# A one-core diffusion-step kernel: two of four latent tiles of the expert layer by a streamed table and dense gates instead of per-token gathers

## The chip, the cores and the metric

The kernel runs on one core of one Trainium2 chip. The metric is device time in microseconds (us), and lower is better. Everything is float32. Three runs of the kernel before gave 2536.47 us (median), 2534.52 and 2538.31.

## The reference, cut to what matters

One layer of a diffusion backbone over 128 context tokens and 512 latent tokens, 1024 wide. A mixing part (a gated recurrence plus attention) adds `y` to `x`; then comes PEER, an expert layer over 16384 experts, which is what the change is about. `w_u` and `w_v` are tables of 16384 rows of 1024 numbers (64 MB each).

```python
def peer(h, w_q, sub_keys, w_u, w_v):            # per block of 128 tokens
    q = (xb @ w_q).reshape(n, P_HEADS, 2, P_QDIM // 2)        # 8 heads
    s = jnp.einsum('nhpd,hpkd->nhpk', q, sub_keys)            # 2 x 128 scores a head
    s1, i1 = lax.top_k(s[:, :, 0], 16)
    s2, i2 = lax.top_k(s[:, :, 1], 16)
    cand_s = s1[..., :, None] + s2[..., None, :]
    cand_i = i1[..., :, None] * 128 + i2[..., None, :]
    top_s, pos = lax.top_k(cand_s, 16)
    idx = jnp.take_along_axis(cand_i, pos, axis=-1)           # 16 experts a head and token
    g = jax.nn.softmax(top_s, axis=-1)
    act = jax.nn.gelu(jnp.einsum('nhkd,nd->nhk', w_u[idx], xb))
    return jnp.einsum('nhk,nhkd->nd', g * act, w_v[idx])
x = x + gate1 * y;  x = x + gate2 * peer(rmsnorm(x) * (1 + scale2) + shift2)
```

A tile is 128 tokens: tile 0 is the context, tiles 1 to 4 are the latents. Each token picks 8 x 16 = 128 experts, so a tile needs 128 "slots" of 128 rows of both tables.

## The kernel before, in words

**Tiles and order.** The program is one hand-ordered stream per engine. `plan_groups` lists every PSUM group (`NAMES`) in the order in which TensorE makes it; the other engines walk the same list. The order is: modulation vectors (`ada`), the context tile's mixing part, its `post(0)`, the latent tiles' projections and mixing (`mix(1)`), then `post(1)` for tile 1 and `post(2)` for tiles 2 to 4. `post` multiplies by `w_out` (groups `y`), normalizes, turns (`x2T`, `h2`), and makes the queries (`qp`) and scores (`ss`) of the 8 heads. PA has four PSUM banks, taken in turn.

**Slots.** A slot is one indirect DMA of 1 MB (`gather`: for each of 128 tokens a row of `u` and a row of `v` side by side, array `uv`), a dot product of the `u` half with the token's `h2` on VectorE (`dot`, L1412), a GELU and a weight on ScalarE (`w_slot`, L957, L963), and an accumulation of the weighted `v` half. For tile 0 the last is a scalar-tensor-tensor on VectorE into PSUM (`v_row`, L1440). For the other tiles TensorE does it: ScalarE makes a diagonal matrix of the weights (L973) and two matmuls of 512 columns add into PSUM (`v_slot`, L600); of tile 1's first 64 slots every second goes this way (`v_odd`, L587). Gathers are issued by GpSimd (L1213, L1235). In all 640 slots.

**Placing.** `Beside` puts slots between the groups of the list at places that `STAGES` sets: tile 0's 128 slots beside projections, attention and `mix(1)`, then 64 slots of tile 1 beside the two posts. The other 448 slots follow in loops with no other work, with eight gather buffers (`GB_`: the three slab slots, HL, and `GA`); beside other work there are four (`GA`) or six (`GC`).

**Routing.** For each head VectorE finds the 16 experts in about 30 small instructions (`route_parts`, L1332 to L1389): two top-16 searches over 128 scores, 54 candidate sums, a third search, and three passes over 128 x 864 elements that turn positions into expert numbers. It is cut into 12 parts laid between the slots (`ROUTE_AT`); after part 7 ScalarE takes the exponentials (L952). `tile_end` adds the result to `x`, normalizes and hands the tile to the output DMA.

**Slabs.** SP streams all weights as slabs of 1 MB through a ring of three (`SLABS`, `NSLAB`); a slab's DMA is issued when the slab three before it has been read.

## Time and profile before

| | before |
|---|---|
| median of 3 runs | 2536.47 us |
| runs | 2534.52 to 2538.31 us |
| profiled execution, span of its records | 2543.3 us |
| busy TensorE / VectorE / ScalarE / GpSimd | 79% / 69% / 37% / 37% |
| DMA moved | 805.53 MB, mean 317 GB/s |

### The profile page before, as it was taken

To read this page: it belongs to the slowest core of one execution; us is meant where nothing else is said; L and a number is where in the kernel's file an instruction comes from. 1 tells how busy PE (TensorE), PEld (TensorE's weight loads), DVE (VectorE), ACT (ScalarE), POOL (GpSimd) and SP (SyncE) were. 2 spreads that over 40 slices of the span, in tenths; PEclk is the share of its full clock that TensorE was granted. 3 is DMA by queue.
4 is the path that set the end of the run, shared out by engine and by line. 5 is a ranking of instruction groups with operands and counts; after the bars stand their busy time and mean duration, and the time that the engine had idled before them with its cause. 6 is when DMAs were issued, how large, how long until landed. Compare 5 with 4: busy or idle time off the path is not lost. (4 is left out here: it accounts for less than half of the span.)

```text
span 2543.3 us, 27323 instructions
## 1 busy us (share of the span) xinstructions
PE 2005.6 (79%) x6925; PEld 1104.9 (43%) x6925; DVE 1749.4 (69%) x3969; ACT 945.2 (37%) x2456; POOL 941.2 (37%) x774
## 2 busy tenths in 40 slices
PE   6978898946677798668698776877768787687876
PEld 2577846745566543267455222322223222232222
DVE  2732278886776678767787777777777777777764
ACT  1402145223343434312333444444444444344443
POOL 0020012232222222303233554656545665456654
PEclk9998999977888899879899998999999999999999
DMA  8744678851111389859798999999999999999997
GB/s 317 289 152 154 231 291 322 332 192 67 67 67 60 150 332 337 337 203 401 272 372 317 422 421 393 420 422 422 421 404 415 422 422 421 407 401 421 422 422 330
DMA packets 113299, 805.53 MB, mean 317 GB/s; under 512 B 12596, under 2 KB 14006, under 8 KB 17046
## 3 DMA queue, kind: packets, MB, share of 16 engines
q0 software_dynamic: 93760, 680.96, 66.5%
q1 hardware_dynamic: 17704, 118.17, 12.6%
q10 hardware_dynamic: 1712, 4.98, 0.5%
q8 instruction: 50, 0.82, 0.1%
q14 instruction: 73, 0.60, 0.1%
HBM read 800.79 MB, written 3.28 MB: 316 GB/s over the span
## 5 line engine op out<-in xcount | busy, mean ns | idle before, releaser
L1213 POOL DMA_INDIRECT RG<-in_uv,idxs x264 | 356.5, 1351 | 562.0 <-DVE pl L1440 322.1
L957 ACT ACTIVATE agel<-apre 128x1 f32<-128x1 f32 x640 | 129.3, 202 | 984.6 <-DVE apre L1412 981.2
L600 PE MATMUL pl<-RG,BP 128*128 128x512 f32 x576 | 294.9, 638 | 106.8 <-ACT BP L973 102.3
L600 PE MATMUL pl<-RING,BP 128*128 128x512 f32 x576 | 281.7, 621 | 62.1 <-ACT BP L973 59.6
L1412 DVE CUSTOM_DVE_ANT_0 R<-RG,AB 128x1024 f32<-128x1024 f32 x201 | 246.8, 1230 | 100.8 <-DMA RG<-in_uv,idxs 79.8
L1213 POOL DMA_INDIRECT RING<-in_uv,idxs x168 | 248.9, 1482 | 158.7 <-PE pl L600 69.4
L1412 DVE CUSTOM_DVE_ANT_0 R<-RING,AB 128x1024 f32<-128x1024 f32 x168 | 205.9, 1226 | 95.6 <-DMA RING<-in_uv,idxs 77.2
L625 PE MATMUL pa<-HL,RING 128*128 128x512 f32 (+2 forms) x800 | 243.7, 461 | 4.2 <-DVEq L457 2.6
L600 PEld LDWEIGHTS pl<-RG,BP 128*128 128x128 f32 x576 | 100.1, 192 | 294.5 <-ACT BP L973 214.0
L973 ACT ACTIVATE BP<-CT,wexp 128x128 f32<-128x128 f32 x480 | 192.7, 401 | 51.1 <-PE pl L600 12.9
L600 PEld LDWEIGHTS pl<-RING,BP 128*128 128x128 f32 x576 | 104.3, 194 | 234.2 <-ACT BP L973 139.7
L963 ACT ACTIVATE wexp<-agel,gws 128x1 f32<-128x1 f32 x640 | 188.7, 295 | 22.4 <-ACT agel L957 0.3
L625 PEld LDWEIGHTS pa<-HL,RING 128*128 128x128 f32 x800 | 134.5, 195 | 106.0 <-issue 74.3
L1213 POOL DMA_INDIRECT EB<-in_uv,idxs x88 | 118.3, 1345 | 147.0 <-DVE pl L1440 96.8
L1440 DVE SCALAR_TENSOR_TENSOR pl<-RG,wexp,pl 128x1024 f32<-128x1024 f32 x118 | 151.6, 1285 | 9.6 <-ACT wexp L963 9.5
L1412 DVE CUSTOM_DVE_ANT_0 R<-RG,BP 128x1024 f32<-128x1024 f32 x96 | 117.7, 1226 | 43.4 <-DMA RG<-in_uv,idxs 27.6
L1412 DVE CUSTOM_DVE_ANT_0 R<-EB,AB 128x1024 f32<-128x1024 f32 x67 | 82.4, 1229 | 60.1 <-DMA EB<-in_uv,idxs 58.0
L625 PE MATMUL pa<-RING,AB 128*128 128x256 f32 (+2 forms) x432 | 103.9, 390 | 14.8 <-DVEq L457 10.3
L600 PE MATMUL pl<-HL,BP 128*128 128x512 f32 x192 | 94.9, 617 | 24.9 <-ACT BP L973 22.2
L957 ACT ACT_TABLE_LOAD x86 | 110.3, 1283 | 9.9 <-ACT RING L1096 2.8
L600 PE MATMUL pl<-EB,BP 128*128 128x512 f32 x192 | 98.8, 639 | 11.1 <-ACT BP L973 11.1
L625 PEld LDWEIGHTS pa<-RING,AB 128*128 128x128 f32 (+1 forms) x432 | 82.9, 201 | 34.1 <-issue 17.3
(288 smaller groups left out, 3261.0 us busy)
## 6 DMA issues: line engine op xcount, KB each, us to landing
RING<-in_in_slabs SPq DMA_DIRECT2D x42, 1024.0 KB, 6.0
RING<-in_pq_slabs SPq DMA_DIRECT2D x24, 1152.0 KB, 5.5
RING<-in_ada_slabs SPq DMA_DIRECT2D x16, 1024.0 KB, 5.0
RING<-in_out_slabs SPq DMA_DIRECT2D x12, 1024.0 KB, 9.1
RG<-in_col_slabs POOLq DMA_DIRECT2D x8, 1024.0 KB, 6.9
RING<-in_o_slabs SPq DMA_DIRECT2D x8, 1024.0 KB
RG<-in_uv,idxs POOLq DMA_INDIRECT x297
RING<-in_uv,idxs POOLq DMA_INDIRECT x168
```

What stands on the lines that cost most here:

```text
L600: last = nc.tensor.matmul(acc[:, c * 512:(c + 1) * 512], DG[:, k % 2, :], bufs[k % len(bufs)][:, D + c * 512:D + (c + 1) * 512], start=Fal ...
L625: return nc.tensor.matmul(out, l, r, start=s, stop=e)
L957: A(agel[:, par, k:k + 1], apre[:, par, k:k + 1], ACT.Gelu).then_inc(gel_done, 1)
L963: A(wexp[:, par, k:k + 1], agel[:, par, k:k + 1], ACT.Copy, scale=gws[:, par, k:k + 1]).then_inc(w_done, 1)
L973: A(DG[:, i % 2, :], ident, ACT.Copy, scale=wexp[:, par, k:k + 1]).then_inc(dg_done, 1)
L1213: nc.gpsimd.indirect_dma_start(out=bufs[b], out_offset=None, in_=uv, in_offset=bass.IndirectOffsetOnAxis(ap=idxs[:, par, k:k + 1], axis=0) ...
L1412: V.tensor_tensor_reduce(out=SCR[k % 2], in0=buf[:, 0:D], in1=hc, scale=1.0, scalar=0.0, op0=ALU.mult, op1=ALU.add, accum_out=apre[:, par, ...
L1440: V.scalar_tensor_tensor(PL[:, :], (GC[i % NGC] if t else GA[n % NGA])[:, D:2 * D], wexp[:, n // TOPK % 2, n % TOPK:n % TOPK + 1], PL[:, : ...
```

## The change

Tiles 0, 1 and 3 keep the gathers. Tiles 2 and 4 are computed densely: for every one of the 16384 experts, whether a token picked it or not.

- **Table.** `u_slabs` and `v_slabs` are the two tables cut into 128 chunks of 128 experts, two chunks to a slab of 1 MB: 64 `dU` and 64 `dV` slabs through the same ring. `experts_u(c)` (group `("U", c)`) multiplies a chunk with the 256 tokens of both tiles (8 matmuls of 256 columns); `gelu_u` puts GELU of it into `AR`, a ring of 50 chunks. `weigh` multiplies 16 chunks by their gates. `experts_v(c)` (`("V", c)`, L994) adds chunk c's part of both outputs into PSUM (4 matmuls of 512 columns).
- **Gates.** The dense gate of (token, expert) is the softmax weight or 0. Sixteen `dense_route` calls (one per head of tiles 2 and 4) are whole routings on VectorE, in a workspace of their own (`WD`, in `mbias`). Then, per token, a one-hot matrix of each slot's first key times its weight (`OH1`, 8 tensor-scalars of 128 x 128 per 8 tokens on GpSimd, `slot_hots`; for every second group of tile 4 on VectorE, `drawn`) and one of its second key (`OH2`, one 128 x 1024 comparison per 8 tokens on VectorE, `gate_hots`) are multiplied on TensorE (groups `G`, four tokens each, 64 groups). ScalarE copies them to staging (`gates_out`) and writes them to an array in HBM (16 DMAs of 1 MB in pieces of 1 KB), from which SP reads 16 blocks of 1 MB back (`gate_slab`).
- **Slots.** 384 instead of 640, all with `v_row` on VectorE; for tiles 1 and 3 it accumulates in SBUF (`ACC`). No diagonal matrices, no slot matmuls, no loops. All gathers have four buffers (`GA`, `GD`).
- **Order.** Tile 0's end now stands ahead of `post(1)`. The posts are for tiles 1, 2 and 3, 4. Scores are copied out of PSUM by ScalarE, not VectorE. Three dense routings stand between the posts, with no slots in `post(1)`; 26 slots beside `post(2)`; 24 beside the new stage `early` (U chunks 0 to 49, all of the gates, 13 dense routings); 206 beside the new stage `dense` (128 V chunks and U chunks 50 to 127). The ends of tiles 3, 2 and 4 follow in a row.
- **Spill.** `x` of tiles 1 to 4 is written to HBM in the posts and read back for the tile's end (`x1s`).

```diff
-NGA, NGC, NGB = 4, 6, 8
+NGA, NGD = 4, 4
+DENSE, GATHERED = (2, 4), (0, 1, 3)
+NCH, NEARLY, NRING = NKEYS, 34, 50
-BATCHES = [(0,), (1,), (2, 3, 4)]
+BATCHES = [(0,), (1, 2), (3, 4)]
...
-          ("post1", 0, {"y": 3.5, "x2T": 2.0, "h2": 2.0, "qp": 2.0, "ss": 1.0}),
-          ("queries1", 4, {"qp": 2.0, "ss": 0.1}),
-          ("post2", 60, {"y": 3.4, "x2T": 2.5, "h2": 2.5, "qp": 5.2, "ss": 1.2}))
+          ("post1", 0, {}),
+          ("post2", 26, {"y": 3.4, "x2T": 2.5, "h2": 2.5, "qp": 5.2, "ss": 1.2}),
+          ("early", 24, {"U": 3.4, "T": 1.0, "G": 1.6}),
+          ("dense", 206, {"V": 1.0, "U": 1.0}))
...
+SLABS += [("dU", p) for p in range(NRING // 2)]
+for _p in range(NCH // 2):
+    SLABS += [("dV", _p)] + ([("dU", _p + NRING // 2)] if _p + NRING // 2 < NCH // 2 else [])
+DENSE_AT = {("U", 2 * (d - NAHEAD)) if d < PH else ("G", 0, 4 * (d - PH)): d for d in range(NAHEAD, 2 * PH)}
...
+            def experts_u(c):
+                w = slab("dU", c // 2)[:, c % 2 * D:(c % 2 + 1) * D]
+                ps = start(("U", c))
+                for k in range(KD):
+                    last = mm(ps[:, 0:DTOK].rearrange("p (t n) -> p t n", t=ND), w[:, k * P:(k + 1) * P],
+                              hTl[:, k, :].rearrange("p (t a n) -> p t a n", t=ND, a=2)[:, :, 1, :], k == 0, k == KD - 1)
...
+            def experts_v(c):
+                w = slab("dV", c // 2)[:, c % 2 * D:(c % 2 + 1) * D]
+                if c % GBLK == 0:
+                    pe.wait_ge(p_done, ND * (c // GBLK + 1))
+                for i in range(ND):
+                    for x in range(2):
+                        last = nc.tensor.matmul(VACC[i][:, x * 512:(x + 1) * 512], AR[:, c % NRING, i * P:(i + 1) * P],
+                                                w[:, x * 512:(x + 1) * 512], start=c == 0, stop=c == NCH - 1,
+                                                skip_group_check=True)
...
+            def dense_route(d):
+                t, h = DHEADS[d]
+                b = 1 if t in BATCHES[1] else 2
+                dve.wait_ge(sc_ready, 2 * PH * b + 2 * h + 2)
+                for i in range(10):
+                    search(WD, t, h, i)
+                    if i == 3 and d % PH:
+                        weights_of(d - 1)
+                    if i == 7:
+                        dve.sem_inc(dlogit_ready, 1)
+                r(V.tensor_reduce(slots_at(d, 2), REQ, AX, ALU.add))
...
+                for x in range(ONEHOT):
+                    at = q * ONEHOT + x
+                    step.post(nc.gpsimd.tensor_scalar(OH1[n % 2][:, x, :], iota_p, SLT[i][:, 0, at:at + 1],
+                                                      SLT[i][:, 2, at:at + 1], ALU.is_equal, ALU.mult))
...
+            tile_end(0)
+            post(1)
+            route(PH, 0, 12)
+            route(PH + 1, 0, EARLY)
+            for d in range(NAHEAD):
+                dense_route(d)
+            beside.open(1)
+            post(2)
+            for name in early_order():
+                if name in DENSE_AT:
+                    dense_route(DENSE_AT[name])
+                if name[0] == "G" and name[2] % 2 == 0:
+                    gate_hots(name[1], name[2] // 2)
```

TensorE at the end of the program: `po` and `pl` are PSUM accumulators, `BP` holds the diagonal matrices, `RING`, `RG`, `HL` and `EB` gather buffers. Before, the last rows of the last loop's tail:

```order
L600 MATMUL pl<-RING,BP 128x512 x6
L600 MATMUL pl<-HL,BP 128x512 x2
L600 MATMUL pl<-RG,BP 128x512 x6
L600 MATMUL pl<-EB,BP 128x512 x2
L894 MATMUL pl<-ZB 128x128 x8
```

In the change, from the middle of the stage `dense` (`AB` is the ring of weighted activations, `RING` the slabs):

```order
L994 MATMUL pl<-RING,AB 128x512 x2
L710 MATMUL pa<-HL,RING 128x256 x16
L994 MATMUL po<-RING,AB 128x512 x2
L994 MATMUL pl<-RING,AB 128x512 x2
L994 MATMUL po<-RING,AB 128x512 x2
L994 MATMUL pl<-RING,AB 128x512 x2
```

A slot no longer has a matmul; two V chunks and two U chunks take turns.

VectorE before, in a gather loop (`ISA` is the dot product and the read of its sum, the rest are parts of a routing):

```order
L1412 ISA R,apre<-HL,AB 128x1024
L1412 ISA apre 128x1
L1375 TENSOR_TENSOR BP<-BP 128x864
L1412 ISA R,apre<-RG,AB 128x1024
L1412 ISA apre 128x1
L1377 TENSOR_REDUCE BP<-BP 128x16
L1379 CAST idxs<-BP 128x16
```

In the change, in the stage `early`, the end of a dense routing (`CT`), a one-hot comparison (`XS`), a slot, and a part of a slot's routing (`BP`):

```order
L1493 TENSOR_SCALAR CT<-CT 128x1
L1495 CAST CT<-CT 128x16
L1496 TENSOR_TENSOR BP<-CT 128x864
L1499 TENSOR_TENSOR BP<-BP,CT 128x864
L1540 TENSOR_REDUCE BP<-BP 128x16
L1567 TENSOR_TENSOR XS<-CT,BP 128x1024
L1593 ISA R,apre<-R,BP 128x1024
L1593 ISA apre 128x1
L1619 SCALAR_TENSOR_TENSOR AB<-R,wexp,AB 128x1024
L1469 TENSOR_TENSOR BP<-BP 128x2x12
```

Dense routings and comparisons stand on VectorE in one piece between slots, and the accumulation (L1619) has moved to VectorE with its sum in SBUF.

## Rows read from the trace of the kernel before

**Rows 1.** The page, 40 slices of 63.6 us each: busy tenths and GB/s.
```profile
PE   6978898946677798668698776877768787687876
DVE  2732278886776678767787777777777777777764
DMA  8744678851111389859798999999999999999997
GB/s 317 289 152 154 231 291 322 332 192 67 67 67 60 150 332 337 337 203 401 272 372 317 422 421 393 420 422 422 421 404 415 422 422 421 407 401 421 422 422 330
```
**Rows 2.** Windows: window, length, then busy us (count) of PE, PEld, DVE, ACT, POOL, PEclk, DMA share, GB/s.
```profile
900.00:1096.00 196.00, 150.69 (x343) 65.44 (x342) 155.70 (x241) 74.27 (x152) 54.80 (x49) 0.90 0.86 326
1144.00:1208.00 64.00, 56.16 (x269) 45.33 (x268) 49.06 (x124) 15.41 (x46) 20.59 (x20) 0.95 0.99 401
1270.00:1330.00 60.00, 60.00 (x207) 35.28 (x206) 49.71 (x114) 19.04 (x58) 19.30 (x18) 1.00 0.96 370
1500.00:2300.00 800.00, 623.41 (x1300) 228.56 (x1300) 585.26 (x1435) 350.19 (x1030) 454.20 (x313) 0.96 1.00 414
```
**Rows 3.** ScalarE groups in the window 1500 to 2300 us: count of slots.
```profile
L957 ACT ACTIVATE agel<-apre 128x1 f32<-128x1 f32 x313 | 63.1, 202 | 381.3 <-DVE apre L1412 380.3
```
**Rows 4.** VectorE timeline: start, us, engine, line, idle before; slots beside `mix(1)`, then end of them.
```profile
1056.06 1.23 DVE L1412 CUSTOM_DVE_ANT_0 R<-RG,BP 128x1024 f32<-128x1024 f32 x1 [1.40 <-DMA RG<-in_uv,idxs]
...
1058.49 1.22 DVE L1412 CUSTOM_DVE_ANT_0 R<-RG,BP 128x1024 f32<-128x1024 f32 x1
...
1094.67 1.23 DVE L1412 CUSTOM_DVE_ANT_0 R<-EB,BP 128x1024 f32<-128x1024 f32 x1 [0.26 <-DVE AB L1683]
...
1100.88 0.42 DVE L1719 TENSOR_TENSOR HG<-pa,G1L 128x256 f32<-128x256 f32 x1 [3.77 <-PE pa L625]
...
1104.33 0.42 DVE L1719 TENSOR_TENSOR HG<-pa,G1L 128x256 f32<-128x256 f32 x1 [2.46 <-PE pa L625]
```
**Rows 5.** TensorE timeline in `mix(1)`: 32 matmul instructions of 512 columns.
```profile
959.51 14.32 PE L625 MATMUL pa<-HL,RING 128*128 128x512 f32 x32 [0.19 <-ACTq L457]
```
**Rows 6.** Lines L1719 and L1744 (first to last start), then score copies of `post(0)`.
```profile
L1719 DVE TENSOR_TENSOR HG<-pa,EB x4: 425/425/426, 266.3 to 276.6; 128x256 f32<-128x256 f32 x4
L1744 DVE COPY R<-pa x32: 278/292/292, 292.5 to 1388.3; 128x128 f32<-128x128 f32 x32
...
302.54 0.29 DVE L1744 COPY R<-pa 128x128 f32<-128x128 f32 x1 [1.72 <-PE pa L625]
304.55 0.29 DVE L1744 COPY R<-pa 128x128 f32<-128x128 f32 x1 [1.72 <-PE pa L625]
```
**Rows 7.** VectorE timeline of a whole routing on its own: first and last of its rows.
```profile
323.14 0.29 DVE L1350 COPY BP<-R 128x256 f32<-128x256 f32 x1
323.58 0.29 DVE L1332 MAX8 BP<-BP 128x8 f32<-128x128 f32 x1
...
336.09 0.23 DVE L1389 TENSOR_SCALAR gws<-BP 128x16 f32<-128x16 f32 x1
```
**Rows 8.** Groups by shape: VectorE over 128x1024, GpSimd over 128x128, gathers by GpSimd.
```profile
L1699 DVE TENSOR_TENSOR AB<-AB,R 128x1024 f32<-128x1024 f32 x4 | 4.9, 1225 | 0.6 <-DVE R L1698 0.3
L1706 DVE SCALAR_TENSOR_TENSOR AB<-AB,st,R 128x1024 f32<-128x1024 f32 x4 | 5.1, 1284 | 1.1 <-DMA R<-in_normf_rows 1.0
L1255 POOL TENSOR_TENSOR HG<-HG 128x128 f32<-128x128 f32 x5 | 2.3, 468 | 0.4
L1213 POOL DMA_INDIRECT RG<-in_uv,idxs x45: 932/1643/1917, 1599.9 to 1882.8; - x45
```
**Rows 9.** Timeline at the end of the program.
```profile
2529.48 1.23 DVE L1412 CUSTOM_DVE_ANT_0 R<-EB,AB 128x1024 f32<-128x1024 f32 x1 [1.22 <-DMA EB<-in_uv,idxs]
2534.30 1.23 DVE L1698 TENSOR_TENSOR R<-pl,G 128x1024 f32<-128x1024 f32 x1 [3.59 <-PE pl L894]
...
2540.24 0.33 SPq L570 DMA_DIRECT2D out<-AB  x1
```

More of the change, by code:

```diff
@@ L78 @@
 EARLY = 6
-FIRST_ODD = 9
 EXPO_AT = 5
@@ L475, in open, with clear @@
             def open(self, t):
-                self.first, self.end = t * TSLOT, min((t + 1) * TSLOT, NSLOT)
+                self.first, self.end = (0, TSLOT) if t == 0 else (TSLOT, NSLOT)
+            def clear(self):
+                while self.next < self.end and self.next % TOPK in (3, 4):
+                    self.slot(self.next)
+                    self.next += 1
             def rest(self):
@@ L1838, in shape_constants @@
+            beside.before(("U", NRING - 4))
+            weigh(0, 0)
+            weigh(0, 1)
+            beside.before(("V", 4))
+            weigh(1, 0)
+            weigh(1, 1)
+            for b in range(2, NBLK):
+                beside.before(("V", GBLK * b - 8))
+                weigh(b, 0)
+                weigh(b, 1)
+            beside.rest()
+            for e in range(2, NT):
+                tile_end(e)
 def shape_constants():
```

775 lines of the change are left out of this document (425 added, 350 removed).

## The prediction, made before the changed kernel was run

> **What bounds the kernel now.** I read the 40 slices first. From slice 23 on, 1400 us into the span, DMA stands at 9 and moves 393 to 422 GB/s, while VectorE and TensorE stand at 7 [rows 1]. Before that no stage holds DMA at its limit for long. The windows say the same in numbers: from 1500 to 2300 us the DMA share is 1.00 at 414 GB/s, TensorE is busy 623 of 800 us and VectorE 585 [rows 2]. In that window 313 slots pass, one per 2.56 us [rows 3], and each is 1.049 MB, so the last 45% of the program is a gather stream and nothing else counts there. The reader should see that taking bytes away pays here, and only as long as the other two engines, at 78% and 73%, don't become the bound. Beside other work the picture is another: from 900 to 1096 us (`mix(1)`, four gather buffers and the slab ring, as in the whole changed kernel) the DMA share is 0.86 at 326 GB/s with no engine over 80%; from 1144 to 1208 us slabs and gathers together reach 401 GB/s at share 0.99; from 1270 to 1330 us TensorE is the bound and DMA moves 370 [rows 2]. These rates price the new stages.
>
> **Bytes.** 256 slots of 1.049 MB go (268 MB). The table brings 128 slabs (134 MB), the gates 16 MB units out and 16 back (34 MB), the spill of x 4 MB. Net 96 MB less; at 414 GB/s that is 232 us, the most the change could give if DMA stayed the bound throughout. It doesn't, so I sum the stages.
>
> **Up to the posts: nothing.** The slots of tile 0 keep their places, so the first `y` matmul of `post(1)` starts where it did, one group ahead of its first reader: 1100.88 - 3.45 = 1097.4 us (the pitch of these groups is 1104.33 - 1100.88) [rows 4]. Tile 0's end now stands ahead of that reader on VectorE: after the last dot product at 1094.67 us [rows 4], one accumulation (1.28) and a tile end, 2540.24 - 2534.30 = 5.9 us [rows 9]. I cost it at nothing: four PSUM banks take four `y` groups, 13.8 us, before TensorE is stopped. Were that cover gone, it would cost 7 us. The removed score copies free VectorE but stand beside TensorE's work: nothing.
>
> **post(1), 106 us.** Eight `y` groups by 3.45: 28. Then norm, turns and first query: in `post(0)` 292.5 - 276.6 = 15.9 us pass from the last `y` to the first score, of which two pitches (4.0) are queries: 12 for one tile [rows 6], 15 for two. A head half of `post(0)` has 16 + 2 instructions of 128 columns in 2.01 us [rows 6], 0.11 each; one of 256 columns takes 3.45/16 = 0.22. So 16 x 0.22 + 4 x 0.11 = 3.9 us, sixteen times: 63. VectorE meanwhile does the first routing of tile 1, half the second and three dense ones. A whole routing alone takes 336.32 - 323.58 = 12.7 us [rows 7]; a dense one lacks a cast, 12.4. That is 57 us beside the 63. Ends at 1203.
>
> **post(2), 118 us.** The same 28 + 15. Beside the queries each pair of head halves needs 1.18 MB of slab and 2.4 gathers, 3.7 MB: 9.3 us at 401 GB/s, against 7.9 of TensorE and, by 3.2 us a slot, 8 of VectorE. A slot alone costs VectorE 1058.49 - 1056.06 = 2.43 us [rows 4]; its share of a routing is 12.5/16 = 0.8. So 75 us, and 1321.
>
> **early, 344 us.** Here VectorE is the bound, and this is the price of the change. Chunks 0 to 9 carry five dense routings (62) and three slots (10): 72, where TensorE needs 35. Tile 2's gates: eight routings (99), sixteen comparisons of 128 x 1024 at 1.23 [rows 8] (20), nine slots (29), turning the slots (3): 151. Tile 4's gates: sixteen comparisons (20), eight drawn pairs at 2.5 (20), eight slots (26): 66, TensorE 62. Then sixteen U chunks by TensorE: 16 x 3.45 = 55. The DMA need (25 slabs, 24 gathers, 16 gate writes) is 65 MB units, 170 us, so half of DMA's time is given away here. The gate writes go in pieces of 1 KB; no row shows such a write, and even at twice the time per byte they hide (16 x 2.6 us more of 170 idle). The Trainium skill ("Perfetto Trace Analysis", DMA Optimizations) says that transfers under 2 KB carry significant overhead each and speaks for larger ones; by it the 170 grow and the sum stays. Ends at 1665.
>
> **dense, 845 us.** 206 gathers less 3 already issued, 100 slabs, 12 gate reads, 2 units of x: 317 x 1.049 = 332 MB. At 401 GB/s 829 us. TensorE: a 512-column instruction takes 14.32/32 = 0.45 us [rows 5], so a V chunk (8) 3.6 and a U chunk 3.45: 128 x 3.6 + 78 x 3.45 = 727. VectorE: 206 x 2.43 + 11 routings (138) + 14 weighings of 2048 columns (34) + one tile end (8) = 681. The accumulation in SBUF instead of PSUM costs no more: 1284 ns with all operands in SBUF [rows 8]. DMA is last, but by 12% only. I add 2 us at each of eight gate blocks, where V waits for `weigh`: 845. Bounds: 332/0.414 = 803 and 332/0.326 = 1020; I take the row in which both queues were backlogged, since three engines with room keep them so. Ends at 2510.
>
> **Tail, 23 us.** Last dot 1.2, accumulation 1.3, three tile ends at 5.9, output 3.1 (2540.24 to the end) [rows 9]; before, it was 2543.3 - 2529.5 = 14.
>
> Sum 1097 + 106 + 118 + 344 + 845 + 23 = 2533 against a span of 2543.3. Measured runs lie 6.8 us under the span: 2527, or 0.4% faster. A 96 MB saving comes to 10 us, because early stands still for DMA. The break-even is dense at 855 us, 389 GB/s.
>
> **Rivals.**
> **1. Coupling (slower).** In dense a slot stands at every chunk, four buffers hold the gathers, and V waits for gates every 16 chunks. Each engine is within 18% of the longest, and a late one holds the rest. For it: in 900 to 1096 us, built the same way, 326 GB/s with room on all engines [rows 2]. Against it: V chunks need no reply from VectorE within a block, and TensorE may run four U groups ahead. At 370 GB/s dense takes 898 us, the kernel 2580; it decides from 389 down. At 326 it would be 2700.
> **2. GpSimd in early (slower).** 192 tensor-scalars of 128 x 128 lie there. The nearest row is 468 ns [rows 8], 3.7 us per 8 tokens, hidden. But a gather's issue spreads from 0.93 to 1.92 us beside VectorE's slots [rows 8]: if each small operation were held 1.0 us so too, 8 tokens take 11.8 us. Tile 2's gates would take 188 + 9 issues of 1.9 = 205 instead of 151, tile 4's 94 + 15 = 109 instead of 66: 97 more, 2624. The Trainium skill ("SBUF — State Buffer", SBUF: two separate sides) says that a VectorE operation with two SBUF inputs and a GpSimd operation that reads SBUF lock each other out for a whole instruction; by it this rival is the rule.
> **3. DMA stays full (faster).** Slabs as large as the gathers at the pure gather rate, 414 GB/s, and no block waits: dense 803, the kernel 2485.
>
> **How the numbers follow.** Forecast 0.48, rival 1 0.22, rival 2 0.12, rival 3 0.18. 0.2% (5 us) is about what a measurement tells from no change. The forecast's own range is 2500 to 2560 (early and posts 15 us either way, dense 829 to 860): 0.34 faster, 0.08 same, 0.06 slower. Rival 3 is faster; rival 1 gives 0.02 to same and 0.20 to slower; rival 2 is slower. Faster 0.52, same 0.10, slower 0.38. The range reaches from below rival 3 (2455, with early 30 us shorter as well) to 2610, past rival 1 at 370 GB/s; the worst of rivals 1 and 2 stay out.
>
> **What would show it.** Right: VectorE at 9 through early and DMA near half; early 330 to 360 us long; in dense a DMA share of 0.97 or more near 400 GB/s, a slot per 4.1 us, TensorE waiting for slabs and VectorE for gathers. Rival 1: DMA share near 0.9, waits of GpSimd on the accumulation and of TensorE on ScalarE or VectorE. Rival 2: GpSimd full in early and TensorE's G groups waiting for it. It would be wrong altogether if the posts, with ScalarE now copying scores, waited for ScalarE, or if a dense routing took longer than 12.4 us for its waits on the exponential.

## The result, and where the time went

| | before | after |
|---|---|---|
| median of the runs | 2535.5 us (2533.6 to 2538.3) | 2725.1 us (2719.5 to 2728.9) |
| profiled span | 2543.3 us | 2727.0 us |

The ratio of after to before is 1.0741, with a 95% interval of 1.0725 to 1.0757. The changed kernel is 7.4% slower. 2527 us and a range up to 2610 were predicted. The bytes came out as reckoned: DMA moved 707.90 MB, 98 MB less than before, where 96 had been forecast. The time did not follow them.

The page of the changed kernel, busy tenths in 40 slices of 68.2 us, answers to [rows 1]:

```profile
PE   6969899566777984956844467899878787879772
DVE  3642388877766887348687765466676867676767
POOL 0020022222221222001207778322222222222221
DMA  8826598721114897435933445689989899999986
GB/s 310 302 104 232 205 361 333 270 73 62 62 62 183 337 342 271 183 134 219 366 107 105 142 162 193 251 323 388 392 345 393 330 397 351 398 360 382 377 337 239
```

The flat row of 9s that the kernel before had is gone. In slices 17 to 19, the posts, DMA is at 3 to 5; in slices 21 to 25, the early stage, at 3 to 5 again, and GpSimd stands at 7 and 8 in slices 22 to 25, while VectorE falls from 8 to 4 (slices 21 to 26). Later DMA comes back to 330 to 398 GB/s, not to 420.

The stages as I had summed them, by first and last instructions in the trace (first reader of `y`, first gelu of a U chunk, first V matmul, last accumulation of a slot):

| | posts | early | dense | from start to posts | tail |
|---|---|---|---|---|---|
| predicted | 224 | 344 | 845 | 1097 | 23 |
| after | 275 | 429 | 911 | 1090 | 22 |
| difference | +51 | +85 | +66 | -7 | -1 |

Three stages miss by 51, 85 and 66 us, and with the other two that is all of the 194 us between a span of 2533 and one of 2727. As forecast, tile 0's end cost nothing (the first reader of `y` comes 3.6 us late behind it, and from the third on VectorE waits for TensorE again), and the tail took 22.

These marks lie later than the prediction's, which counts a stage from its first matmul. TensorE's first `y` matmul is at 1079.7 us, its first U matmul at 1347.7, while ScalarE stood for a dense routing (8.3 us) before its exponential and came to the first gelu only at 1365.0:

```profile
1347.70 13.98 PE L710 MATMUL pa<-HL,RING 128*128 128x256 f32 x64
```

By the prediction's own marks the start is 18 us early, the posts take 268 us (44 over) and early 446 (102 over); the sum is the same. The first reader of `y` lies anywhere between 1088 and 1104 us in the profiles of this kernel and of its variants, none of which differs before it, so a shift of the start by 15 us means nothing.

**The posts.** VectorE's waits from 1125 to 1240 us, TensorE's from 1187 to 1300:

```profile
DVE BP L1514 <- ACT BP L1063: 40.9, 1, 40.9
DVE BP L1459 <- ACTq L530: 14.2, 1, 14.2
...
PE pa L710 <- DVEq L530: 35.0, 1, 35.0
PE pa L713 <- DVEq L530: 17.0, 1, 17.0
```

L1514 is part 11 of the first gathered routing of tile 1, L1063 its exponential. The two timelines, VectorE's and ScalarE's, show why it is late:

```profile
1187.27 0.16 DVE L1514 RECIPROCAL BP<-BP 128x1 f32<-128x1 f32 x1 [40.93 <-ACT BP L1063]
...
1185.09 0.27 ACT L1257 ACTIVATE AB<-pa 128x128 f32<-128x128 f32 x1
1185.54 1.28 ACT L1063 ACT_TABLE_LOAD   x1 [0.17 <-ACT AB L1257]
1186.84 0.31 ACT L1063 ACTIVATE BP<-BP 128x16 f32<-128x16 f32 x1
```

The exponential stands in ScalarE's program behind all 16 query and score groups of `post(1)`, of which the last copy (L1257) is at 1185.09. VectorE reached it at 1146 and stood still. Its three dense routings, which I had laid beside TensorE's queries, then came after the queries; TensorE made the first four `y` groups of `post(2)`, one for each bank, and waited 35.0 us for VectorE to read them.

**Early.** Windows: chunks 0 to 9, tile 2's gates, tile 4's gates, the last sixteen U chunks. Columns as in [rows 2].

```profile
1363.00:1440.00 77.00, 27.83 (x99) 22.45 (x99) 62.32 (x216) 20.92 (x39) 10.44 (x13) 0.71 0.31 109
1440.00:1610.00 170.00, 97.68 (x483) 87.81 (x483) 126.31 (x340) 53.41 (x97) 126.81 (x128) 0.79 0.41 135
1610.00:1735.00 125.00, 76.83 (x400) 70.70 (x401) 66.05 (x81) 26.03 (x55) 96.95 (x72) 0.80 0.54 179
1735.00:1793.00 58.00, 58.00 (x270) 51.07 (x269) 22.51 (x30) 9.01 (x27) 5.76 (x5) 1.00 0.82 313
```

I had 72, 151, 66 and 55. Two thirds of the excess is in tile 4's gates (59 of 86 us), where VectorE, said to be the bound, is busy 66 of 125 us and GpSimd 97. The one-hots that GpSimd scales, by source line (shortest, median and longest ns, first and last start):

```profile
L1384 POOL TENSOR_SCALAR EB<-CT,BP x128: 780/791/2544, 1433.1 to 1597.7; 128x128 f32<-128x128 f32 x128
L1384 POOL TENSOR_SCALAR EB<-CT,RW x64: 785/1402/2542, 1610.9 to 1724.8; 128x128 f32<-128x128 f32 x64
```

GpSimd's timeline, one piece in each part:

```profile
1468.12 7.98 POOL L1384 TENSOR_SCALAR EB<-CT,BP 128x128 f32<-128x128 f32 x8
...
1625.68 10.87 POOL L1384 TENSOR_SCALAR EB<-CT,RW 128x128 f32<-128x128 f32 x8 [2.08 <-PE pa L710]
1637.45 1.02 POOL L1371 DMA_INDIRECT R<-in_uv,idxs  x1 [0.91 <-POOL EB L1384]
```

One takes 0.78 us at least, where I had 0.47 from the nearest row; eight take 7.98 us beside the end of one slot and a routing's small instructions, and 10.87 beside comparisons and a slot, all of 1024 columns. TensorE waits 48.3 us in eight pieces for GpSimd in 1600 to 1735.

A second price hangs on these waits. TensorE does the `G` groups of tile 4 in eight pieces of four groups, 32 matmul instructions each. Two of them:

```profile
1621.79 6.74 PE L710 MATMUL pa<-XS,EB 128*128 128x128 f32 x32 [11.93 <-POOLq L530]
1681.73 3.84 PE L710 MATMUL pa<-XS,EB 128*128 128x128 f32 x32 [1.55 <-POOLq L530]
```

After the wait of 11.9 us the granted clock was 0.53 over the piece (1621.8 to 1628.3), close to the lower of its two levels, 1.2 GHz; after the wait of 1.55 it was 1.00. Seven of the eight pieces follow waits of 4.7 to 11.9 us and take 5.3 to 6.7 us. All eight take 45.9 us, where 3.84 each would be 31: 15 us more, in the same chain with GpSimd's pieces. The forecast priced TensorE at its full clock everywhere.

**Dense.** Two windows, same columns:

```profile
1850.00:2100.00 250.00, 219.65 (x727) 142.35 (x726) 173.68 (x301) 47.26 (x156) 55.82 (x55) 0.95 0.96 378
2100.00:2450.00 350.00, 282.93 (x920) 180.27 (x918) 258.29 (x440) 63.66 (x213) 88.21 (x79) 0.95 0.95 368
```

DMA moves 368 to 378 GB/s, not 401; over the whole stage 332 MB in 911 us are 365. No engine is full. The waits in 1850 to 2450 us form a circle: GpSimd waits for VectorE's accumulation, VectorE for gathers, and TensorE for ScalarE.

```profile
POOL R L1371 <- DVE AB L1619: 328.5, 97, 11.9
POOL AB L1371 <- DVE AB L1619: 112.3, 31, 5.9
...
DVE R L1593 <- DMA R<-in_uv,idxs: 90.0, 48, 4.1
DVE R L1593 <- issue: 36.3, 19, 3.8
DVE R L1593 <- DMA AB<-in_uv,idxs: 20.0, 13, 4.2
...
PE pa L710 <- ACTq L530: 89.6, 35, 10.0
```

From this profile alone one can't say which link of it is the tight one.

### The profile page after: what moved, and what is told of

It is laid out like the page before. It is cut to its first block, busy times and chain, and to the rows that moved or that the text cites. A ratio compares the mean times of both kernels' runs of the same rounds, so it can differ in the third digit from the quotient of the medians.

```text
span 2727.0 us, 28055 instructions
## 1 busy us (share of the span) xinstructions
PE 2068.6 (76%) x8515; PEld 1459.6 (54%) x8515; DVE 1809.1 (66%) x3622; ACT 701.7 (26%) x1719; POOL 714.1 (26%) x713
## 2 busy tenths in 40 slices
DMA packets 114558, 707.90 MB, mean 260 GB/s; under 512 B 11140, under 2 KB 28934, under 8 KB 32614
## 4 chain that ended last, share of the span: by engine, by line
DMA 27%; DVE 26%; PE 21%; issue 16%; POOL 7%; ACT 2%; DVEq 1%; POOLq 0%; ACTq 0%; SPq 0%
DMA R<-in_uv,idxs 21%; PE pa L710 18%; POOL EB L1384 6%; DVE AB L1619 5%; DVE pl L1619 4%; DMA AB<-in_uv,idxs 3%; DVE AB L1584 2%; PE po L710 1%; PE pa L713 1%; DVE AB L1748 1%; DVE AB L1756 1%; DMA EB<-in_uv,idxs 1%; DMA RING<-in_ada_slabs 1%; DVE BP L1499 1%; DVE BP L1496 1%
## 5 line engine op out<-in xcount | busy, mean ns | idle before, releaser
L710 PE MATMUL pa<-HL,RING 128*128 128x256 f32 (+1 forms) x2848 | 731.2, 416 | 120.6 <-ACTq L530 116.5
L710 PEld LDWEIGHTS pa<-HL,RING 128*128 128x128 f32 x2848 | 557.5, 199 | 294.4 <-issue 222.0
L1371 POOL DMA_INDIRECT R<-in_uv,idxs x288 | 322.2, 1119 | 1150.5 <-DVE AB L1619 736.0
L1593 DVE CUSTOM_DVE_ANT_0 R<-R,BP 128x1024 f32<-128x1024 f32 x192 | 235.5, 1227 | 134.6 <-DMA R<-in_uv,idxs 90.6
L1619 DVE SCALAR_TENSOR_TENSOR AB<-R,wexp,AB 128x1024 f32<-128x1024 f32 x192 | 246.0, 1281 | 54.4 <-ACT wexp L1081 54.2
L994 PE MATMUL po<-RING,AB 128*128 128x512 f32 x512 | 244.3, 600 | 39.6 <-DVEq L1586 39.6
L994 PE MATMUL pl<-RING,AB 128*128 128x512 f32 x512 | 243.0, 597 | 0.0
L710 PE MATMUL pa<-RING,AB 128*128 128x256 f32 (+3 forms) x528 | 125.0, 386 | 80.8 <-DVEq L530 77.1
L994 PEld LDWEIGHTS po<-RING,AB 128*128 128x128 f32 x512 | 98.1, 192 | 147.1 <-issue 145.0
L994 PEld LDWEIGHTS pl<-RING,AB 128*128 128x128 f32 x512 | 98.5, 192 | 124.6 <-issue 124.6
L1384 POOL TENSOR_SCALAR EB<-CT,BP 128x128 f32<-128x128 f32 x128 | 124.8, 984 | 18.7 <-PE pa L710 16.9
L1371 POOL DMA_INDIRECT AB<-in_uv,idxs x64 | 63.6, 994 | 251.6 <-DVE AB L1619 243.0
L1619 DVE SCALAR_TENSOR_TENSOR pl<-R,wexp,pl 128x1024 f32<-128x1024 f32 x96 | 123.3, 1285 | 5.5 <-ACT wexp L1081 5.3
```

The costliest lines, as they stand in the source:

```text
L710: return nc.tensor.matmul(out, l, r, start=s, stop=e)
L994: last = nc.tensor.matmul(VACC[i][:, x * 512:(x + 1) * 512], AR[:, c % NRING, i * P:(i + 1) * P], w[:, x * 512:(x + 1) * 512], start=c == ...
L1371: nc.gpsimd.indirect_dma_start(out=bufs[b], out_offset=None, in_=uv, in_offset=bass.IndirectOffsetOnAxis(ap=idxs[:, par, k:k + 1], axis=0) ...
L1384: step.post(nc.gpsimd.tensor_scalar(OH1[n % 2][:, x, :], iota_p, SLT[i][:, 0, at:at + 1], SLT[i][:, 2, at:at + 1], ALU.is_equal, ALU.mult))
L1593: V.tensor_tensor_reduce(out=SCR[k % 2], in0=bufs[b][:, 0:D], in1=hc, scale=1.0, scalar=0.0, op0=ALU.mult, op1=ALU.add, accum_out=apre[:, ...
L1619: V.scalar_tensor_tensor(acc, (GD[(n - TSLOT) % NGD] if s else GA[n % NGA])[:, D:2 * D], wexp[:, n // TOPK % 2, n % TOPK:n % TOPK + 1], ac ...
```

## The experiments

All stand on the changed kernel unless said otherwise. Stage lengths in us, by the same marks:

| run | posts | early | dense | median | to before (95%) |
|---|---|---|---|---|---|
| after | 275 | 429 | 911 | 2725.1 | 1.0725 to 1.0757 |
| e1_expos | 232 | 433 | 910 | 2694.6 | 1.059 to 1.065 |
| e2_hots | 275 | 399 | 902 | 2695.5 | 1.059 to 1.066 |
| e3_noslots | 273 | 363 | 992 | 2742.3 | 1.077 to 1.083 |
| e4_small_slabs | 271 | 434 | 809 | 2634.8 | 1.033 to 1.040 |
| e5_pattern | 274 | 428 | 912 | 2729.4 | 1.066 to 1.077 |
| e6_few_rows | 274 | 435 | 789 | 2613.4 | 1.023 to 1.031 |
| e7_light_pe | 273 | 435 | 913 | 2739.6 | 1.072 to 1.081 |
| e8_light_dve | 276 | 429 | 848 | 2671.0 | 1.046 to 1.055 |
| e9_ring42 | 275 | 423 | 907 | 2724.5 | 1.072 to 1.076 |
| e10_five | 273 | 421 | 842 | 2653.3 | 1.044 to 1.048 |
| e11_combo | 235 | 399 | 907 | 2660.0 | 1.046 to 1.050 |
| e12_all | 230 | 388 | 843 | 2588.0 | 1.018 to 1.024 |
| e13_half_pool | 272 | 379 | 902 | 2673.0 | 1.050 to 1.057 |
| e14_scalar_hots | 235 | 381 | 841 | 2579.6 | 1.013 to 1.019 |
| e15_scalar_hots_split | 234 | 373 | 847 | 2570.2 | 1.008 to 1.015 |
| e16_more_early | 237 | 401 | 803 | 2559.3 | 1.006 to 1.010 |
| e17_eight_early | 235 | 384 | 822 | 2559.1 | 1.008 to 1.012 |

### The posts: e1_expos

```diff
                 for m in range(2 * PH):
+                    if b == 1 and m in (6, 11, 15):
+                        x = (6, 11, 15).index(m)
+                        expos(PH) if x == 0 else dense_expos(x - 1)
                     ps = group(("qp", b, m))
...
-            expos(PH)
-            for d in range(NAHEAD):
+            for d in range(2, NAHEAD):
                 dense_expos(d)
```

> Correct kernel. ScalarE takes the exponential of the first gathered routing after post(1)'s sixth query group and those of the first two dense routings after the 11th and 15th, instead of all of them after the 16 groups. Theory (the wait of VectorE on ScalarE between the posts is on the path: 40.9 us at 1187, after which TensorE waits 35.0 us at 1233 for VectorE): post(2) starts about 35 to 40 us earlier, the stages behind it keep their lengths, and the time falls by 30 to 45 us, to about 2685. Rival (the wait only hides work that has to be done anyway, and post(2) or the early stage takes it back): the time falls by under 10 us. Second rival: ScalarE now stands still in post(1) for the logits, and post(1) becomes longer by what it waits, so that the gain is 15 to 25 us.

Measured: 31 us less, the posts 43 us shorter, early and dense as long as before within 4 us. (Between the two profiled spans, 2727.0 and 2695.3, the difference to 43 is a start 8 us later and 4 us in early.) VectorE's waits from 1130 to 1240 us, TensorE's from 1190 to 1290, in the new profile:

```profile
DVE BP L1462 <- ACTq L531: 13.3, 1, 13.3
DVE st L1654 <- ACTq L531: 2.7, 1, 2.7
DVE BP L1517 <- ACT BP L1064: 1.2, 1, 1.2
...
PE pa L714 <- DVEq L531: 15.0, 1, 15.0
PE pa L711 <- ACTq L531: 1.5, 2, 0.9
```

The wait of 40.9 is 1.2 and TensorE's 35.0 is gone. What is left of the posts, 232, is 8 from the 224 predicted; by the prediction's marks it is 226 (1087.7 to 1313.8 us). The theory stands.

### Early: e2_hots, e3_noslots, e5_pattern, e13_half_pool

e2: VectorE makes all first one-hots of tile 4.

```diff
-            return i == ND - 1 and q % 2 == 1
+            return i == ND - 1
```

> Correct kernel. All of tile 4's first one-hots (16 groups of 8 tokens) are made by VectorE, where the change has GpSimd make every second group; GpSimd's 64 instructions that took 1.40 us on average are gone, VectorE gets 8 more pairs of 1.25 and 1.36 us, 21 us. Theory (GpSimd sets the pace of tile 4's gates, 122 us long): VectorE then is busy some 87 us there, TensorE 77, and the stage takes 90 to 100 us; the time falls by 22 to 32 us. Rival (the pace there is set by the slots in VectorE's order and their gathers, GpSimd only follows): the stage gets 15 to 20 us longer, and the time with it.

Measured: 30 us less. Tile 4's gates, from first comparison to last gate copy, go from 121 to 89 us. The window over them in e2, beside the third of the windows of early above:

```profile
1617.00:1706.00 89.00, 67.86 (x387) 61.15 (x388) 81.58 (x92) 25.23 (x54) 8.80 (x7) 0.87 0.65 220
```

VectorE is now busy 82 of 89 us: this is the stage as I had meant it, only with more work on VectorE. GpSimd had been the pace. TensorE gains too: its waits are short, the granted clock is 0.87 instead of 0.80, and it is busy 68 us instead of 77.

e3: no slot in early, 230 in dense (the count of `early` in `STAGES` 0, of `dense` 230).

> Correct kernel. No slot lies in the early stage; its 24 go to the dense stage (230 instead of 206). Theory (GpSimd's scalings are slow because VectorE works beside them on two operands from SBUF; alone one takes 0.79 us): without the slots GpSimd's mean stays above 1.0 us in tile 2's gates, since the comparisons of VectorE remain, and falls in tile 4's; the early stage gets 40 to 70 us shorter (VectorE loses 24 slots of 2.5 us and their waits), and the dense stage longer by 24 slots of 4.4 us, 106, so the time rises by 35 to 65 us. Rival (the dense stage is bound by DMA at its own rate, and 24 MB more cost 24 x 1.05 MB / 0.401 = 63 us there): the time is the same within 15 us.

Measured: 17 us more, under the theory's 35 to 65 and just past the rival's 15. Early is 65 us shorter, so a slot costs 2.7 us there, and dense 81 us longer, 3.4 a slot. Slots aren't cheaper in early than 2.7, although DMA is idle half the time. GpSimd's mean goes from 1.40 to 1.18 us in tile 4's gates, as expected; in tile 2's it goes from 0.98 to 0.95, so it was never above the 1.0 that the expectation names.

e5: the same number of drawn groups, in another pattern.

```diff
-            return i == ND - 1 and q % 2 == 1
+            return i == ND - 1 and q % 4 in (1, 2)
```

> Correct kernel. In tile 4's gates VectorE makes the first one-hots of the groups of tokens 1, 2, 5, 6, 9, 10, 13, 14 instead of 1, 3, 5, ...: as many as before on either engine, but GpSimd's eight now fall on both buffers instead of always on the same one. Theory (the price of tile 4's gates is a chain in series: 8 scalings of GpSimd, 10.9 us, then the 4 us in which TensorE reads that buffer, eight times 15): GpSimd's work overlaps TensorE's, the stage falls from 121 us to 85 to 100, and the time by 20 to 35 us. Rival (GpSimd's sum, 89 us busy with the gathers' issues, and its lock-outs by VectorE set the pace whatever the buffers): the stage keeps 110 us or more, and the time falls by under 10 us.

A miss for the theory, as its rival had it: 2729.4 us, no change (121 to 115 us in that part). Its timeline shows GpSimd's two pieces of eight now one after the other, with the wait for TensorE between them:

```profile
1620.82 10.83 POOL L1388 TENSOR_SCALAR EB<-CT,RW 128x128 f32<-128x128 f32 x8 [11.41 <-ACTq L530]
1632.56 1.01 POOL L1375 DMA_INDIRECT R<-in_uv,idxs  x1 [0.91 <-POOL EB L1388]
1638.48 10.45 POOL L1388 TENSOR_SCALAR EB<-CT,RW 128x128 f32<-128x128 f32 x8 [4.91 <-PE pa L714]
```

So the price isn't the order in which the two buffers are filled. GpSimd's piece takes 10.5 to 10.9 us in either order.

e13: GpSimd makes 4 of each 8.

> The output is not the reference's: GpSimd makes only every second of its scaled one-hots (96 of 192), the others keep what stood in the buffer; all else is the changed kernel. It asks what GpSimd's work costs in each part of early. Theory (GpSimd's 8 scalings, 7.8 us per 8 tokens in tile 2's gates, run against VectorE's 9 us and the two are coupled through two buffers; in tile 4's they stand in series with TensorE's reading, 10.9 + 4): tile 2's gates fall from 162 us (first to last comparison 151.6) by 10 to 25 us, since VectorE's 148 us stay, and tile 4's from 121 to 85 to 95; the time falls by 40 to 60 us. Rival (in tile 2's gates GpSimd is hidden and VectorE alone is the pace): only tile 4's part falls, and the time by 25 to 35 us.

Measured: 52 us less. Tile 2's gates, from their first comparison to the first of tile 4's, go from 165 to 154 us; tile 4's, from there to the last gate copy, from 121 to 83. Both fell, as the theory has it: half of GpSimd's work costs 11 us in tile 2's gates and 38 in tile 4's. The 38 hold the clock's part as well: over tile 4's gates the granted clock rises from 0.80 to 0.90, and TensorE is busy 64 us instead of 77. With that half gone, tile 2's part is at 154, against 151 predicted from VectorE's sum.

### Dense: e4_small_slabs, e6_few_rows, e7_light_pe, e8_light_dve

e4 and e6 bring less of each slab of the dense stage:

```diff
+                if kind == "dV" or (kind == "dU" and key[1] >= NRING // 2):
+                    at, src = at[0:8], src[0:8]
```

(e4: `[:, 0:SLAB // 4]` instead.)

> The output is not the reference's: the slabs of the tables that the dense stage reads (all of V's, and U's last 39) bring only the first quarter of their columns, the rest of each buffer keeps what was there; every instruction, wait and gather remains. 103 MB of the dense stage's 340 shrink to 27 MB. Theory (the coupling of VectorE's slots, ScalarE's order and the gathers' four buffers sets the pace, the queues only follow): the dense stage of 911 us keeps 850 us or more, and the time falls by under 60 us. Rival (the DMA engines are the bound, at a lower rate for slabs and gathers mixed than for gathers alone): the stage goes in proportion to its bytes until TensorE, 711 us busy, or VectorE, 655, bounds it, to 720 to 780 us; the time falls by 130 to 190 us.

> The output is not the reference's: the slabs that the dense stage reads bring 8 of their 128 partitions, in full rows of 8 KB (with a quarter of the columns for all partitions the DMA share had stayed at 0.88 at 320 GB/s, since the pieces became 2 KB). 97 MB of the dense stage's 340 go. Theory (what is left when DMA is no bound is TensorE's 3.44 us per V and U chunk in the first part, 537 us, VectorE's some 3.9 us per slot in the V-only part, about 190, and their coupling): V's first to last matmul takes 740 to 785 us instead of 882, the DMA share falls below 0.75, and the time falls by 95 to 145 us. Rival (the coupling alone is the pace, the quarter slabs gained by something else): under 60 us.

Measured: 90 and 112 us less. e4 lies between its two theories; its DMA share stayed at 0.87 to 0.89 with fewer bytes. I had put that down to its rows of 2 KB, but e6, with full rows of 8 KB, stays at 0.84 to 0.88 too, so in neither run is DMA clearly out of the way. e6, with 97 MB less, takes 789 us in dense, and there TensorE is full in the first part (DMA share 0.88 at 313 GB/s):

```profile
1850.00:2100.00 250.00, 250.00 (x875) 165.99 (x874) 207.47 (x362) 55.05 (x182) 78.22 (x70) 1.00 0.88 313
```

Taking 29% of the bytes away shortens the stage by 13%. So transfers are a part of the pace, and not the whole. The share stayed above the 0.75 that I had set.

e7 takes TensorE's work away, e8 part of VectorE's:

```diff
-  VACC[i][:, x * 512:(x + 1) * 512], ... w[:, x * 512:(x + 1) * 512]
+  VACC[i][:, x * 512:x * 512 + 128], ... w[:, x * 512:x * 512 + 128]
-                for k in range(KD):
+                for k in range(KD) if c < NRING else (0, KD - 1):
```

```diff
+                w = D if n < NSLOT - 206 else D // 2
-                ... in0=bufs[b][:, 0:D], in1=hc, ...
+                ... in0=bufs[b][:, 0:w], in1=hc[:, 0:w], ...
```

(in e8 the accumulation likewise.)

> The output is not the reference's: in the dense stage each V matmul does 128 columns instead of 512 and each U chunk 2 of its 8 products, so that TensorE's work there falls from 711 us to under 250; all waits, slabs and gathers remain. Theory (DMA is the bound, and TensorE's bursts at 1.00 together with ScalarE's order keep it from 414 GB/s): the stage runs at 395 to 414 GB/s and falls from 911 to 830 to 865 us, the time by 45 to 80 us. Rival (VectorE with its slots, routings and weighings, coupled to the gathers' four buffers, sets the pace): the stage keeps 890 us or more, and the time falls by under 20 us.

> The output is not the reference's: the slots of the dense stage dot and accumulate 512 instead of 1024 columns, so that VectorE's work there falls by 206 x 2 x 0.6 = 250 us of 655; gathers, slabs and waits remain. Theory (the gathers' four buffers turn faster, the queue is never short of them, DMA is the bound at 400 to 414 GB/s, TensorE waits less for ScalarE): the stage falls from 911 to 830 to 860 us, the time by 50 to 80 us. Rival (the rate of slabs and gathers mixed is 365 GB/s whoever waits, or TensorE is the cause): the time falls by under 20 us.

The same windows of e7, then of e8:

```profile
1850.00:2100.00 250.00, 100.19 (x338) 79.70 (x336) 174.81 (x307) 44.45 (x152) 62.86 (x57) 0.60 0.93 370
2100.00:2450.00 350.00, 139.00 (x476) 111.82 (x476) 251.85 (x441) 66.95 (x218) 89.51 (x80) 0.59 0.91 363
```

```profile
1850.00:2100.00 250.00, 235.49 (x804) 153.99 (x803) 122.62 (x326) 49.97 (x166) 57.31 (x60) 0.98 1.00 411
2100.00:2450.00 350.00, 303.80 (x979) 189.64 (x978) 188.18 (x472) 70.27 (x231) 81.32 (x86) 0.96 0.98 397
```

These two say whose work it is. With TensorE busy 239 instead of 503 of the 600 us the stage keeps its length, 913 us, and its 363 to 370 GB/s: TensorE's work isn't the pace (although its granted clock fell to 0.6), and for e7 the rival was right. Its waits for ScalarE remain, 361 us in e7 instead of 90, so e7 doesn't take the path over ScalarE's order out of the circle. With slots half as wide on VectorE, the bytes unchanged, DMA is at 0.98 to 1.00 with 397 to 411 GB/s and the stage takes 848 us, which is what I had predicted for it, 845. What kept DMA at 365 GB/s was tied to VectorE's time per slot, though VectorE was idle for over a quarter of these 600 us (432 busy; 311 in e8).

### The gathers' buffers: e9_ring42, e10_five

VectorE's work enters twice: it takes time, and it holds buffers. In 2100 to 2450 us a gather was issued each 350/77 = 4.5 us, and four buffers make a turn of 18.2; gathers landed 8 to 9.5 us after their issue, and the rest of the turn is VectorE's order: two slots, a part of a routing, sometimes a block's two weighings (3.6 us for each 2048 columns). If that is the circle, a fifth buffer breaks it without touching any engine. The ring of hidden chunks gives up 8 of 50 places for it.

```diff
-NCH, NEARLY, NRING = NKEYS, 34, 50
+NCH, NEARLY, NRING, NTOP = NKEYS, 34, 42, 50
-        GD = GA[:3] + [view(ABH, NRING * DTOK + 3 * D, 2 * D)]
+        GD = GA[:3] + [view(ABH, NTOP * DTOK + 3 * D, 2 * D), view(ABH, NRING * DTOK, 2 * D)]
```

(e9 has the first edit and four buffers; e10 uses the fifth from slot 180 on, after the staging that lies there has gone out.)

> Correct kernel. The ring of hidden chunks has 42 places instead of 50, so 8 U chunks and their 4 slabs move from the end of early into the dense stage; the gathers' buffers are four as before. It is the control for e10_five. Theory (dense is bound by VectorE's slots with their gathers, as the half-width slots showed, while TensorE has room there): early's last part falls from 60 to 32 us and the dense stage takes 4.2 MB more, 10 to 12 us, so the time falls by 10 to 20 us. Rival (TensorE's work comes back one for one in the dense stage): the time is the same within 5 us.

> Correct kernel. As e9_ring42, with the freed place as a fifth buffer for the gathers from slot 180 on. Theory (VectorE at 3.2 us of work a slot and gathers that land after 9.5 us are tied together by four buffers: with half-width slots on VectorE the stage ran at 397 to 411 GB/s and took 848 us, just what bytes at 401 GB/s give): a fifth buffer loosens this, the dense stage runs at 385 to 400 GB/s and takes 25 to 50 us less than in e9_ring42. Rival (VectorE's own work and its long pieces, 7.3 us for two weighings, set the pace, and buffers don't matter): under 10 us less than e9_ring42.

Measured: e9 2724.5, no change (its rival), e10 2653.3, 71 us less, more than the 25 to 50 expected. e10's windows:

```profile
1850.00:2100.00 250.00, 234.77 (x800) 153.87 (x799) 186.84 (x330) 50.53 (x167) 66.28 (x62) 0.98 1.00 409
2100.00:2450.00 350.00, 319.77 (x1068) 207.21 (x1067) 277.75 (x474) 71.75 (x235) 98.74 (x84) 0.97 0.99 406
```

Against [rows 2], where the pure gather stream had share 1.00 at 414 GB/s, this is nearly the same stream, with VectorE at its full work. The dense stage takes 842 us. One buffer of 8 KB a partition gives back all of its 66 us, with 4 MB more to bring (e9, the control, has the same bytes and 907 us). TensorE's waits for ScalarE fall with it, from 79 us in e9 to 43.

### Together: e11_combo, e12_all

> Correct kernel. The edits of e1_expos and e2_hots together. Theory (the two losses lie in different stages, one between the posts, one in tile 4's gates, and add): 31 + 30, so the time is 2660 to 2670 us. Rival (what is gained early only makes the dense stage start earlier against the same stream and is partly given back): 2680 or more.

> Correct kernel. The edits of e1_expos, e2_hots and e10_five together. Theory: the gains add, 31 + 30 + some 15 for the shorter ring + 25 to 50 for the fifth buffer: 2600 to 2625 us, still slower than the kernel before. Rival (no gain from the buffer): 2645 to 2665 us.

2660.0 and 2588.0: the gains add. e12 is 12 us better than the best expected, since the buffer brings 65 to 71 where 25 to 50 were reckoned, while the shorter ring brings nothing. Posts 230, dense 843, against 224 and 845: two of three stages are as predicted. The 388 us of early stay. The shorter ring had given 6 us there instead of 28 (e9): the last gate copy comes 388 us after the first gelu instead of 367. Two more slots lie beside the gates, 19 instead of 17, which is 5 us at 2.7 each; what the other 16 are is open.

### What is left of early: e14 to e17

e14 stands on e12_all. The second one-hots come from ScalarE:

```diff
+                    step.post(A(OH2[n % 2][:, x, :], iota_p, ACT.Abs, scale=-1.0, bias=SLT[i][:, 1, at:at + 1]))
...
+                    step.post(A(OH2[n % 2][:, x, :], OH2[n % 2][:, x, :], ACT.Relu, scale=-1.0, bias=1.0))
-                step(V.tensor_tensor(OH2[n % 2], keys, slot_row(1), ALU.is_equal), oh2_ready)
```

e15 also has `return i == ND - 1 or q % 4 == 3` in `drawn`. e16 and e17 place 40 and 32 slots in early, most of the added ones beside tile 4's gates and the last U chunks, and 190 and 198 in dense.

> Correct kernel. On top of e12_all, ScalarE makes the second one-hots, as relu(1 - |iota - key|) in 16 instructions of 128 x 128 per 8 tokens, in place of VectorE's comparison of 128 x 1024. Theory (early is bound by VectorE and GpSimd, which also hold each other, while ScalarE is busy 53 of 183 and 27 of 98 us there): at some 0.27 us an instruction (its copies of 128 x 128) ScalarE gets 4.3 us per 8 tokens, 138 in all, and fits; VectorE loses 40 us, and early falls by 25 to 45 us; the time is 2545 to 2565 us. Rival (ScalarE's order, which also serves the slots and the gate copies, becomes the new pace): the time is 2590 us or more.

> Correct kernel. As e14_scalar_hots, and VectorE also makes the scaled one-hots of every fourth group of 8 tokens of tile 2 (4 x 2.6 us), so that GpSimd has 96 instead of 128 instructions there. Theory (after e14 GpSimd, 129 us in tile 2's gates, is the longest there): that part falls by another 10 to 20 us against e14, and the time is 2530 to 2555 us, level with the kernel before. Rival (VectorE's additional 10 us and its lock-outs take it back): within 5 us of e14 or above.

> Correct kernel. As e15_scalar_hots_split, and 40 instead of 24 slots lie in early, most of the added ones beside tile 4's gates (VectorE was busy 59 of 100 us there) and the last U chunks; 190 instead of 206 lie in dense. The dense stage there stands at DMA share 0.97 to 0.99. Theory (dense is bound by bytes now, 16 slots are 16.8 MB or 42 us at 400 GB/s; early, where DMA stands below 0.5, has room on VectorE for 10 or so of them and grows by 10 to 25 us): the time falls by 15 to 30 us against e15, to 2540 to 2555 us. Rival (early is held by the chain of its engines and each slot costs its full 2.5 us and more there, 40 us): within 8 us of e15, 2570.

> Correct kernel. As e16_more_early with 32 slots in early and 198 in dense. Theory: half of e16's gain, the time 2550 to 2562 us. Rival: no gain, or as in e16 where early pays for its slots in full.

e14 gains 8 us and e15 18 against e12, less than the 25 to 45 expected of the first in early alone, and both end above the times that they were expected to reach. ScalarE got 133 us for it, as reckoned, and in tile 2's gates three engines now stand side by side (e14):

```profile
1397.00:1550.00 153.00, 86.45 (x427) 77.56 (x428) 112.63 (x351) 109.25 (x332) 118.51 (x129) 0.76 0.41 141
```

With VectorE's comparisons gone GpSimd's mean fell from 0.97 to 0.93 us, and its 118 of 153 us are the largest sum. e17 and e16 lengthen early by 11 and 28 us against e15, 1.4 and 1.7 us a slot (for the sixteen of e16 the theory had 10 to 25 us, its rival 40), and shorten dense by 25 and 44, some 2.9 a slot. Both end at 2559 us. For e17 that is inside its range, for e16 above its 2540 to 2555; and a gain over e15 isn't clear of noise, since the intervals against the kernel before overlap (1.008 to 1.015 for e15, 1.006 to 1.010 for e16). The best of them is still 0.8% over the kernel before (1.006 to 1.010).

## Why the prediction was wrong

**The sum's price for the posts** failed in one sentence: "VectorE meanwhile does the first routing of tile 1, half the second and three dense ones ... That is 57 us beside the 63." I had counted VectorE's instructions and not asked where ScalarE's program has the exponential that the first of these routings waits for. Posts that wait for ScalarE were among the last conditions named, under which the forecast "would be wrong altogether". e1_expos gives back 43 of 51 us, or 42 of 44 by the prediction's marks. That what is left fits so well is partly luck: in `post(2)` of e1 30 us pass from the last `y` to the first score, 15.0 of them the wait for the norm, where I had 15 for all; and the queries take 66 us where I had 75.

**Early** was priced by VectorE alone, with VectorE "at 9 through early" as the sign of being right; it went from 8 down to 4. "Tile 4's gates: ... 66, TensorE 62" took 121 us. The step that failed is the choice between forecast and rival 2: "The nearest row is 468 ns [rows 8], 3.7 us per 8 tokens, hidden" failed, and GpSimd's scaling costs 0.98 us in tile 2's gates and 1.40 in tile 4's, the second near the 1.47 of the rival. Rival 2's 109 for tile 4's gates was near; its 205 for tile 2's was too much (165), since most scalings there took 0.79. By the run with half of GpSimd's work, at least 38 us of tile 4's excess and 11 of tile 2's hang on GpSimd (e13). Part of the 38 is what TensorE lost at the lower clock after its waits for GpSimd, a term that neither the sum nor a rival had. The Trainium skill ("SBUF — State Buffer", SBUF: two separate sides) states that a VectorE operation with two inputs in SBUF and a GpSimd one that reads SBUF lock each other out for a whole instruction. The trace agrees in direction: eight scalings take 7.98 us beside mostly small instructions and 10.87 beside those of 1024 columns, and the means fall when slots or comparisons go (e3, e14). That the lock is the cause of each long one isn't isolated by a run.

**The gate writes** in pieces of 1 KB did hide, as said: 16 of them, landing 4.9 us after issue by the median. The Trainium skill ("Perfetto Trace Analysis", DMA Optimizations) has transfers under 2 KB as costly. The DMA rows of 1440 to 1740 us have them on a queue of their own (q10), beside gathers (q0) and slabs (q1): packets, MB, share of the window's time of all 16 engines.

```profile
q10 hardware_dynamic: 16784, 17.30, 17.1%
q0 software_dynamic: 2304, 16.78, 16.9%
q1 hardware_dynamic: 1660, 12.16, 12.6%
```

Per MB that is 0.99% for the pieces of 1 KB, 1.01% for the gathers and 1.04% for the slabs. So here, with DMA idle half the time, the trace doesn't agree: no overhead shows, and nothing of the double time that I had allowed. What such pieces cost beside a full queue no run shows.

**Dense** went rival 1's way, at 365 GB/s where I had named 370. The failing step is "DMA is last, but by 12% only" with "three engines with room keep them so". The sums of the work were right within 4%: in the trace TensorE is busy 746 us (not the 711 that two expectations name) and VectorE 655, where the forecast had 727 and 681, and bytes at 401 GB/s give 829. But with four buffers VectorE's time per slot and the gather's 8 to 9.5 us to landing stand partly in series, so the stage is longer than its longest sum. e8 and e10 remove this by VectorE or by a buffer, and both give 842 to 848, the forecast's 845. Rival 1's signs were there, GpSimd waiting for the accumulation and TensorE for ScalarE, but its picture of engines that hold each other in turn was wider than what is shown: TensorE's work had no part in it (e7), and whether ScalarE's order is a link by itself no run says. The 2 us at each gate block were another miss without weight: at two blocks after 2490 us TensorE waits 39.6 us for `weigh`, and 19.1 in e10. Of its evidence, 326 GB/s in 900 to 1096 us [rows 2] with four buffers, I took the number for a far bound, and it was a sign.

**The range** left out that two rivals could come true together, and the posts' wait as well. In the sizes measured, dense's 66 us alone give 2593 and the posts' 51 give 2578, both within 2610; early's 85 alone give 2612, just outside; together they are far out. The step from span to run, 6.8 us down, had the wrong sign besides: in the profiled run of the changed kernel the time, 2728.85 us, is 1.9 above the span.

Left open: of early's 85 us, 49 at least are GpSimd's (e13). The other 36 aren't assigned. The lower granted clock is the rival that was left untested: 0.71 to 0.80 over early's first three windows, and in tile 2's gates too four `G` groups take 5.4 us after a wait; no run changes the clock and nothing else. In e14 and e15 all engines have room and wait for each other, and no run takes one of those waits away by itself.

## What to carry to other kernels

A stage isn't priced by the longest of its engines' sums when a few buffers pass work around a ring: compare the turn of the buffers (count times pitch) with landing time plus the time that the consumer's program holds them, and buy a buffer before work is moved. When work is placed beside other work, follow each of its replies to the line in the other engine's program at which it is given; a reply behind a loop comes when the loop is done. And if several rivals have different stages, their prices add. Last, a wait of TensorE can cost more than its own length, if the granted clock is low when it goes on.
